# 512-token stages: input in rows of 512 columns at one remainder, and the feed-forwards' up tiles as two matmuls of 256 columns

## The reference

```python
def swiglu(x, w_in, w_out):
    gate, up = jnp.split(x @ w_in, 2, axis=-1)      # w_in: 1024 x 5632
    return (jax.nn.silu(gate) * up) @ w_out         # w_out: 2816 x 1024
...
    qkv = x @ w_qkv                                 # 1024 x 3072
...
    kv = x @ kv_w                                   # 1024 x 2048
    q = (x @ w_q).reshape(b, nc, CHUNK, B_HEADS, B_HEAD_DIM)   # 1024 x 1024
```

## Time and profile before

| | us |
|---|---|
| median of three runs | 2580.22 |
| lowest and highest | 2575.26, 2580.89 |
| span of the profiled execution, first to last instruction | 2574.9 |
| PE busy in it | 2530.5 (98%) |
| PEld busy in it | 2296.3 (89%) |

### The profile page before, as it was taken

The page is one execution under the profiler, slowest core; times in us unless marked ns, Lnnn a source line. Parts: engine busy times, 40 slices in busy tenths (PEclk is TensorE's granted clock), DMA queues, the critical chain, the costliest instruction groups (busy, mean ns, idle before and its releaser), DMA issues.

```text
span 2574.9 us, 44715 instructions
## 1 busy us (share of the span) xinstructions
PE 2530.5 (98%) x19246; PEld 2296.3 (89%) x19246; DVE 1622.4 (63%) x2784; ACT 1163.6 (45%) x1924; POOL 168.7 (7%) x218
## 2 busy tenths in 40 slices
PE   9999999999999999999999999999999999999998
PEld 7777889889887888989899899999999989999998
DVE  6767756457566655546766556666675754766666
ACT  4554534335555443334554444434444534544443
POOL 0000200100100010110000011001000000200100
PEclk9999999999999999999999999999999999999999
DMA  5221954974312492795411149359652112954975
GB/s 193 88 64 70 256 148 154 296 186 148 113 65 82 144 246 86 263 259 162 149 67 67 63 142 265 96 166 292 157 186 97 67 62 104 260 145 135 294 176 162
DMA packets 104279, 397.39 MB, mean 154 GB/s; under 512 B 10400, under 2 KB 12704, under 8 KB 84240
## 3 DMA queue, kind: packets, MB, share of 16 engines
q1 hardware_dynamic: 60400, 249.07, 28.2%
q0 software_dynamic: 42960, 143.88, 23.7%
q10 hardware_dynamic: 720, 1.57, 0.2%
HBM read 383.87 MB, written 133.30 MB: 201 GB/s over the span
## 4 chain that ended last, share of the span: by engine, by line
PE 90%; DVE 6%; ACT 3%; DMA 1%; issue 1%; DVEq 0%; ACTq 0%; SPq 0%
PE P L700 60%; PE P L1030 13%; PE P L818 4%; PE P L796 3%; PE P L707 2%; DVE WL L2131 2%; PE P L830 1%; ACT WH L1489 1%; DMA raw<-in_wts 1%; PE P L1127 1%; PE P L1148 1%; PE P L1240 1%; PE P L844 1%; PE P L876 1%; DVE X L2226 0%
## 5 line engine op out<-in xcount | busy, mean ns | idle before, releaser
L700 PE MATMUL P<-XH,WL 128*128 128x256 f32 (+3 forms) x3080 | 841.8, 322 | 14.8 <-DVE XL L2462 6.9
L700 PE MATMUL P<-XL,WH 128*128 128x256 f32 (+3 forms) x3080 | 822.6, 316 | 0.0
L700 PE MATMUL P<-XH,WH 128*128 128x256 f32 (+3 forms) x3080 | 819.4, 315 | 0.0
L2131 DVE TENSOR_TENSOR WL<-raw,WH 128x1024 fp32r<-128x1024 f32 (+2 forms) x533 | 573.5, 1078 | 325.0 <-ACT WH L1489 323.5
L1489 ACT ACTIVATE WH<-raw 128x1024 fp32r<-128x1024 f32 (+2 forms) x533 | 498.0, 941 | 470.3 <-PE P L700 228.8
L700 PEld LDWEIGHTS P<-XH,WL 128*128 128x128 f32 x3080 | 517.2, 188 | 63.9 <-DVE XL L2462 9.8
L700 PEld LDWEIGHTS P<-XH,WH 128*128 128x128 f32 x3080 | 516.2, 188 | 38.1
L700 PEld LDWEIGHTS P<-XL,WH 128*128 128x128 f32 x3080 | 515.3, 188 | 36.8
L1030 PE MATMUL P<-GHH,WL 128*128 128x272 f32 (+1 forms) x616 | 177.6, 288 | 9.5 <-DVE WL L2131 9.5
L1030 PE MATMUL P<-GHH,WH 128*128 128x272 f32 (+1 forms) x616 | 176.3, 286 | 0.0
L1030 PE MATMUL P<-GHL,WH 128*128 128x272 f32 (+1 forms) x616 | 176.2, 286 | 0.0
(11 more groups left out here) (372 smaller groups left out, 3787.4 us busy)
## 6 DMA issues: line engine op xcount, KB each, us to landing
raw<-in_wts SPq DMA_DIRECT2D x151, 1024.0 KB, 5.0
sums<-in_quads POOLq DMA_DIRECT2D x32, 1152.0 KB, 28.9
sums<-in_quads POOLq DMA_DIRECT2D x32, 960.0 KB, 24.3
sums<-in_quads POOLq DMA_DIRECT2D x16, 1536.0 KB, 19.1
raw<-sums SPq DMA_DIRECT2D x64, 384.0 KB, 3.4
sums<-in_quads POOLq DMA_DIRECT2D x16, 1280.0 KB, 13.1
raw<-sums SPq DMA_DIRECT2D x64, 320.0 KB, 3.1
raw<-in_wts SPq DMA_DIRECT2D x48, 384.0 KB, 3.5
```

Source lines behind the costliest of these rows:

```text
L700: ins = nc.tensor.matmul(P[:, a:a + x1 - x0], wb[:, s, 128 * k:128 * k + 128], xb[:, kx, x0 - c0:x1 - c0], start=start and i == 0, stop=st ...
L2131: nc.vector.tensor_tensor(WL[:, u % NS, 0:length(u)], raw_of(u), WH[:, u % NS, 0:length(u)].bitcast(F), ALU.subtract).then_inc(*dve.up("wl ...
```

## The change

Four tables of offsets, one pair for each of the four 512-token inputs: version 0 is the input of attention a, 1 of f0, 2 of attention b, 3 of f1. Each of the eight rows now has 512 columns (2,048 bytes, a multiple of 256), laid one behind the other in the same `XH` and `XL` at 16, 0, 48 and 48 columns from the start. That puts all rows of an input at one remainder of 256 bytes: 192, 128, 64 and 64. All readers and writers of these inputs follow through `xh`, `xl` and `rows`; the inputs of the 528-token stages stay as they were. And the 41 up units in each feed-forward that were 24 matmuls of 512 columns are now 48 of 256, both halves of a product behind each other.

```diff
+IN_HIGH = (16, 0, 48, 48)
+IN_LOW = (16, 0, 48, 48)
...
+        def row(f, at, k, a, b):
+            return f[:, at + 512 * k + a - META:at + 512 * k + b - META]
+
+        def xh(ver, k, a, b):
+            return row(in_high, IN_HIGH[ver], k, a, b) if ver < 4 else XH[:, k, a:b]
...
+            return (*(f[:, at:at + 4096].rearrange("p (k t) -> p k t", t=512)
+                      for f, at in ((in_high, IN_HIGH[ver]), (in_low, IN_LOW[ver]))), META)
...
+            def tile_of_halves(u, b, hi, lo):
+                pe.wait_ge(*at("wlo", u))
+                for k in range(8):
+                    for i, (wb, xb) in enumerate(((WL, hi), (WH, lo), (WH, hi))):
+                        for n in range(2):
+                            ins = nc.tensor.matmul(P[:, 512 * b + 256 * n:512 * b + 256 * n + 256],
+                                                   wb[:, u % NS, 128 * k:128 * k + 128], xb[:, k, 256 * n:256 * n + 256],
+                                                   start=n == 0 and k == 0 and i == 0, stop=k == 7 and i == 2, skip_group_check=True)
+                ins.then_inc(*pe.up("unit", u))
...
             def feed_forward(l, between):
...
+                hi, lo, c = rows(1 + 2 * l)
                 for n in range(2 * NF):
...
                     if n >= 3:
                         take(b)
-                        tile(up_unit(U, n), one(b), XH, XL)
+                        tile_of_halves(up_unit(U, n), b, hi, lo)
...
             def layer_a():
                 U = first["a"]
+                hi, lo, c = rows(0)
...
-                        tile(U + 6 * g + n, one(b), XH, XL, slot)
+                        tile(U + 6 * g + n, one(b), hi, lo, slot, c)
...
             def norm_result(s, m, hf):
...
-                nc.scalar.activation(XH[:, m, a:b], tmp[m % 4][:, a:b], ACT.Identity, bias=...
+                nc.scalar.activation(xh(s + 1, m, a, b), tmp[m % 4][:, a:b], ACT.Identity, bias=...
```

More of the change, by code:

```diff
@@ L373, in build, with xl, rows @@
         XL = sb("XL", [128, 8, T], R)
+        in_high, in_low = (f[:, :, :].rearrange("p k t -> p (k t)") for f in (XH, XL))
+        def row(f, at, k, a, b):
+            return f[:, at + 512 * k + a - META:at + 512 * k + b - META]
+        def xh(ver, k, a, b):
+            return row(in_high, IN_HIGH[ver], k, a, b) if ver < 4 else XH[:, k, a:b]
+        def xl(ver, k, a, b):
+            return row(in_low, IN_LOW[ver], k, a, b) if ver < 4 else XL[:, k, a:b]
+        def rows(ver):
+            if ver >= 4:
+                return XH, XL, 0
+            return (*(f[:, at:at + 4096].rearrange("p (k t) -> p k t", t=512)
+                      for f, at in ((in_high, IN_HIGH[ver]), (in_low, IN_LOW[ver]))), META)
         raw = sb("raw", [128, RAW, 2048])
@@ L721, in early @@
                         pe.wait_ge(*at("xl", 0, k))
-                        ins = part(u + n, k, regions[n], XH, XL, k, 0, k == 0, k == 7)
+                        ins = part(u + n, k, regions[n], hi, lo, k, c, k == 0, k == 7)
                     ins.then_inc(*pe.up("unit", u + n))
             def early_halves(u, seg, ver, one_bank, between, late=()):
+                hi, lo, c = rows(ver)
                 pe.wait_ge(*at("wlo", u))
@@ L739, in early_halves @@
                 for k in range(8):
-                    part(u + 2, k, [seg(2, 0)], XH, XL, k, 0, k == 0, k == 7, True)
+                    part(u + 2, k, [seg(2, 0)], hi, lo, k, c, k == 0, k == 7, True)
                     between(1, k)
@@ L746, in early_halves @@
                         for n in ns:
-                            ins = part(u + n, k, [seg(n, 1)], XH, XL, k, 0, k == 0 and not one_bank, k == 7, True)
+                            ins = part(u + n, k, [seg(n, 1)], hi, lo, k, c, k == 0 and not one_bank, k == 7, True)
                             if k == 7:
@@ L807, in values_of @@
             def values_of(layer, g, u, slot):
+                hi, lo, c = rows(2 * layer)
                 pe.wait_ge(*at("wlo", u))
@@ L816, in values_of @@
                             o = P[:, 512 * b + 256 * n:512 * b + 256 * n + 256]
-                            for i, (xb, wb) in enumerate(((XL, WH), (XH, WL), (XH, WH))):
-                                ins = nc.tensor.matmul(o, xb[:, k, c0:c1], wb[:, (u + k // 4) % NS, 256 * (k % 4):256 * (k % 4) + 256],
+                            for i, (xb, wb) in enumerate(((lo, WH), (hi, WL), (hi, WH))):
+                                ins = nc.tensor.matmul(o, xb[:, k, c0 - c:c1 - c], wb[:, (u + k // 4) % NS, 256 * (k % 4):256 * (k % 4) + 256],
                                                        start=n == 0 and k == 0 and i == 0, stop=k == 7 and i == 2,
@@ L1175, in layer_b @@
                 work = Threads()
+                hi, lo, c = rows(2)
                 def slot(k):
@@ L1590, in norm_result @@
                 act.wait_ge(*at("nrm", s, m, hf))
-                nc.scalar.activation(XH[:, m, a:b], tmp[m % 4][:, a:b], ACT.Identity, bias=par("ln_b", 16 * (s // 2) + 8 * (s % 2) + m)
+                nc.scalar.activation(xh(s + 1, m, a, b), tmp[m % 4][:, a:b], ACT.Identity, bias=par("ln_b", 16 * (s // 2) + 8 * (s % 2) + m)
                                      ).then_inc(*act.up("xh", s + 1, m, hf))
@@ L1708, in feed @@
                 act.wait_ge(*at("rnm", s, m, hf))
-                nc.scalar.activation(XH[:, m, a:b], tmp[m % 4][:, a:b], ACT.Copy).then_inc(*act.up("xh", s + 1, m, hf))
+                nc.scalar.activation(xh(s + 1, m, a, b), tmp[m % 4][:, a:b], ACT.Copy).then_inc(*act.up("xh", s + 1, m, hf))
             def feed_forward(l):
@@ L2097, in act_program @@
                 act.wait_ge(x_loaded[k], 16)
-                nc.scalar.activation(XH[:, k, C1], X[:, k, C1], ACT.Copy).then_inc(*act.up("xh", 0, k))
+                nc.scalar.activation(xh(0, k, META, T), X[:, k, C1], ACT.Copy).then_inc(*act.up("xh", 0, k))
                 if k == 2:
```

26 lines of the change are left out of this document (13 added, 13 removed).

## The result

| | before | changed |
|---|---|---|
| median, us | 2577.12 (20 runs) | 2584.45 (20 runs) |
| lowest and highest | 2573.46, 2580.89 | 2577.24, 2593.26 |
| span of the profiled execution | 2574.9 | 2580.2 |

The changed kernel takes 1.0027 times as long, with a 95% interval of 1.0021 to 1.0032: about 7 us more, where 1.5 less was forecast. Its times are also spread over 16.0 us, those of the kernel before over 7.4.

The account below looks back on a forecast made before the run. PE was taken as the bound (busy 98%), paced by matmul start distances. Terms -4.9 + 4.2 - 0.8 + 0.6 + 0.3 - 0.9 = -1.5 us gave 2578.7 us against the median, range 2568 to 2588.

Parts of the forecast that it names:

- the case that was held likeliest: Feed-forwards' up tiles: f1 at the fast pace, f0 ordinary at 118 or 120 ns; chance 0.55, range 2574 to 2584.
- f1's up tiles: 984 pairs of halves at 64 against 128 enter and keep the fast pace, 226.7 for 231.7 ns: -4.9 us.
- f0's up tiles: 984 pairs of halves at 128 against 128, taken at 118 ns a matmul: +4.2 us, ends -4.9 and +8.2.
- the two direct rows: Two short trace rows at 128 against 128, five distances each: 120 and 116 ns a matmul.
- third rival: f0's up tiles cost +8.2 in place of +4.2, f1 fast: 2582.7 us; shares the chance of 0.55.
- All pauses in the down projections are followed by the fast pace: Argument against the rival that neither feed-forward's up tiles reach the fast pace (2588.3 us, chance 0.18).
- `values_of`, -0.8: Attention a's first call at 113.3 ns, -0.4 us; its other three calls, -0.4; attention b unchanged at 117.9 ns.
- Projections: Attentions' 512-wide projections: b at 233.5 ns, +0.6 us; a between 231.7 and 233.5, +0.3 us.
- Halves of the first three units: About 100 halves in each of b and f1 go from 118 to 113.3 ns: -0.9 us.
- they stay: In f0 the halves of the first three units keep their pace of 118 ns.

Follow-up runs that it names:

- halves alone: The kernel before, rows of 528 columns, with both feed-forwards' up tiles as two matmuls of 256 columns: 2586.44 us, 1.0034 of before.
- the fastest kernel: The changed kernel with whole 512-column up tiles, both feed-forwards' inputs at remainder 128 and both attentions' at 192: 2564.43 us, 0.9949 of before.

## Why the prediction was wrong, by its steps

The forecast was 1.5 us less; measured are 7.3 us more. The median lies inside the stated range and in the case that was held likeliest, but the direction is wrong.

**f1's up tiles: right.** 113.3 ns from the first to the last, -2.5 and -2.4 us, together -4.9, as forecast.

**f0's up tiles: the step that failed.** The mechanism was named (128 against 128 has no quick pace), its size was not: the term took 118 ns, "the middle of the two direct rows", and it measured 120.0: +8.2, not +4.2. The earlier trace rows had said 120 and the earlier trace rows 116. Both rows have stream and stationary operand at 128, but the earlier trace rows has one row k of halves between rows at other remainders, where the first distances still belong to the neighbours; the earlier trace rows is no longer, yet it was the one that was right. The averaging had no ground. (The text ahead of the prediction says that the half beginning at column 272 lies 64 bytes further. It lies 256 columns, 1,024 bytes, further, and so at the same remainder; the earlier trace rows is rightly taken as 128. The kernel with halves alone bears it out: in its rows k = 2, at 64, both halves come down to 113.3 ns.) The listed third rival, "f0 at 120 ns and f1 fast", is what happened in the up tiles, and its 2582.7 is 1.7 below the median measured.

**"All pauses in the down projections are followed by the fast pace": false.** This sentence carried the assumption that the down phases stay as they were. In 12 profiles of all kernels here, 25 of 48 down phases ran at 113.3 and 23 at 117.8. In the kernel before it was 7 of 8, so its one profile made a draw look like a rule; in the changed one 3 of 8. At 1.6 us one slow phase, less a wait that is 0.3 shorter, stands behind the +1.3 of the table, and four slow phases would be 6.7. The prediction had no term for them.

**The wait at f0's second up stretch: not foreseen.** +1.2 us in the profile. It was 1.7 us where it had been 0.5. It showed again in the second profile of the changed kernel (1.5 us), with the weights at 192 (2.1) and with f1 at 128 (2.7); but also in one of the two executions of the fastest kernel (1.6, and none in the other), whose f0 runs at its best. So f0's slower up tiles aren't needed for it. Whether they make it likelier is not shown: all three profiles with f0 at 120.0 have it, and two of the nine others. What is late is a weight unit's transfer; what delays it was not followed up.

**`values_of`, -0.8: about right, by two errors.** Attention b stayed at 117.8, as said. In attention a the first call, for which the prediction took the quick pace from end to end, was slow. Its first and last row in the changed kernel, 94 distances:

```profile
32.39 0.28 PE L851 MATMUL P<-WH,XL 128*128 128x256 f32 x1
...
43.46 0.28 PE L851 MATMUL P<-WL,XH 128*128 128x256 f32 x1
```

11.07 us, 117.8 ns, where 10.65 us were foretold. In the second profile of the same kernel it was 113.6. The other three calls, taken at 1.5 ns a matmul, gained more: over their distances between 100 and 300 ns the mean fell from 121.6 to 118.8, about -0.8 us where -0.4 was foretold. The model (the difference decides, with the roles turned round as well) was right; the assumption that the pace is then known was not.

**Projections: right in b, sign wrong in a.** b came out at 233.1 to 233.5, as taken from the output projection. a (192 against 128) was taken between 231.7 and 233.5 and is at 228.9 to 229.5: about -1.0 us in place of +0.3. The two ends were both from other differences; nothing in the trace bounded this one from below.

**Halves of the first three units: half of the -0.9.** From a stage's first start to its first whole unit it is 0.3 us less in b and 0.3 less in f1. In f0, for which the prediction wrote "they stay", it is 0.2 more: those halves went to difference 0 and 120.0 ns as well.

**The sum.** f0's two up stretches +8.4 and f1's -5.2 (their first units included), attention a -1.5, the wait +1.2, the slow down phase +1.3, attention b and its output +0.5, the second block, which the change does not touch, +0.6: +5.3 us, which is the difference of the two spans. Against the medians it is 7.3. The 2 us between may be further slow phases, as in the second profile; I can't show that for runs without a profile. The same goes for the wider spread of the changed kernel's times: it has 1,968 matmuls more that can take either pace (8.9 us between all quick and all slow), and its times spread over 8.6 us more. This is argued, not shown.

**The rule that spoke against the change.** The rows here put a pair at +8.3 ns in f0 and -5.0 in f1 against the one matmul. The Trainium skill, page "TensorE: Matmul & The Clock Gate", section "Back-to-back issue gap", gives N / 2.4 + 2.5 ns as the gap of a single matmul, by which a pair costs 2.5 ns more everywhere (an estimate from the page: +4.9 us in all). Its sign is that of the result. This case's traces disagree with the rule behind it: 256 columns took 113.3 to 120.0 ns where it gives 109.2, 512 took 226.7 to 233.3 where it gives 215.8, and the pair was dearer at one difference and cheaper at another.

**What stays open.** Why the difference of remainders matters at all; what draws 113.3 or 117.8 at a pause (the same program got both, and neither the pause's length nor the pace ahead of it settles it); why up stretches at -64 were quick in 13 of 14 cases and down phases in 25 of 48; and whether the kernels are alike in this. 7 of 8 quick phases in the kernel before and 7 of 8 in the fastest, against 11 of 32 in all the others, look unlike, but this is too few to say so.

## What to carry to other kernels

Before a stream of matmuls is split or its operands are moved, measure its pace from start to start at the exact pair of remainders and the exact width that it will have: here the best placement for 512 columns (both operands at one remainder) was the worst for 256. Prefer a placement with one pace to one with a better and a worse one: whole matmuls at difference 0 and halves at -64 both reach 226.7 ns for 512 columns, but only the first did so every time (10 stretches of 10, against 13 of 14). And a pace seen in one profile is one draw: a second profile of the unchanged kernel would have shown that the down phases are no constant.

## What the runs showed of the hardware that I had not expected

- The distance between successive float32r matmuls depends on the difference of the two operands' start addresses, modulo 256 bytes: 113.3 to 120.0 ns for 256 columns, 226.7 to 233.3 for 512. It doesn't depend on the absolute address as far as tried (128/128 and 192/192 agree, 64/128 and 128/192 agree; f0 at an offset of 0 and of 64 columns, 256 bytes apart, has 226.7 both times), and it holds when the roles are exchanged. Only remainders that are multiples of 64 were tried.
- The order is different for the two widths: difference 0 is slowest at 256 columns (120.0) and quickest at 512 (226.7).
- At -64 a stream of 256 columns has two stable paces, 113.3 and 117.8 ns. No steady stretch was seen to change its pace without a pause in it; one of 113 us kept the slow one to its end. The pause can be short: in the second profile of the changed kernel a single distance of 216 ns, at 654.83 us in attention b's first units, stands between 113.3 and 117.8.
